# The first feed-forward as seven block products, with the conditioning sums in 512-wide halves

## The chip, the cores and the metric

The kernel runs on one core of a Trainium2 chip. The metric is the device time of one execution in microseconds; single executions are compared by their medians. All numbers below come from one profiled execution of the kernel before, or are stated to come from the timed runs.

## The reference

Two transformer-like blocks work on one sequence of 512 tokens with 1024 features, all in float32. What this case touches is the first block: a conditioning vector `c` is turned into scales, shifts and gates by two layers of weights, and each layer has a feed-forward with 4096 hidden features.

```python
c_act = jax.nn.silu(c)
for i in range(DEPTH):                      # two layers
    mod = c_act @ ada_w[i] + ada_b[i]       # (1024) @ (1024 x 6144)
    sh1, sc1, g1, sh2, sc2, g2 = jnp.split(mod[:, None, :], 6, axis=-1)
    h = rmsnorm(x, norm_g[i, 0]) * (1.0 + sc1) + sh1
    y = mlstm_mixer(h, ...) if i == 0 else sgu_mixer(h, ...)
    x = x + g1 * rmsnorm(y, norm_g[i, 1])
    h = rmsnorm(x, norm_g[i, 2]) * (1.0 + sc2) + sh2
    y = jnp.square(jax.nn.relu(h @ ffn_w1[i])) @ ffn_w2[i]   # 4096 hidden
    x = x + g2 * rmsnorm(y, norm_g[i, 3])
```

Behind it stand a second block (two kinds of attention, a convolutional feed-forward) and a last norm, which the change leaves as they are.

## The kernel before

Float32 products are made from two parts: every operand is split into a high part (`fp32r`) and a rest, and a product of 128x128 by 128x512 takes three matmuls (high x high, high x rest, rest x high). A weight tile of 1 MB lands in `raw`; ScalarE copies it to a high part (`w_both_hi` or `u_both_hi`), VectorE subtracts to get the rest (`..._lo`), and only then TensorE may use it.

The phases stand in a row: `a_in`, the mixer, `a_out`, **ffn0**, `b_in`, `b_out`, **ffn1**, and the second block. There is no scheduler: each engine has its own program written out by hand, in one fixed order, and semaphores tie the programs together. An engine that waits holds back all that stands behind it in its program, DMA issues included.

**ffn0** goes through the 4096 hidden features in four groups of 1024. A group has four weight tiles up (192 matmuls), and four down, in two pairs (`tok_pair`, 192 matmuls). ScalarE squares the rectified hidden block, VectorE makes its rest.

**ffn1** treats its first three groups (`FAST` = 3) another way. The four tiles up are the same (`fast_up`, 192 matmuls, L1264). The product down is cut into 2x2 blocks, and seven block products (`fast_product`, L1282, 168 matmuls) stand for the eight. The operands are sums: T1 = B11+B12 and others of the weights, made by VectorE in the raw tile (`fast_sum`, L2818) and once by an accumulating DMA of GpSimd; S1 to S4 of the hidden blocks, made by VectorE in `s_sum` and `s3_sum` (L2810, L2835, L2844, L2849). Each sum is then split by ScalarE (`fast_a`, L1956; `fast_hi`, L1931) and VectorE (`fast_a_lo`, L2805; `fast_lo`, L2799). The results are added into `Y` by VectorE (`fast_add`, L2829), and the PSUM bank of a product is free only when it has been added. The second product of a group (m = 1) needs both halves of S1, which need the last hidden block of the group. Its order on VectorE is: rest of B11, T1, rest of the first hidden quarter, S3, rest of S3, first half of S1, its rest, rest of T1 (operand 5), T2, second half of S1, its rest. The fourth group of 1024 is done the plain way.

**The conditioning** (`ada`): 48 slices of 256 columns. Slices 20 to 47 (28 slices, in 7 rounds of four) are made during ffn0. ScalarE's program issues a load of 1 MB into the one buffer `ada_raw` (`ada_in`, L1522) when the slice before has been summed; VectorE multiplies and adds eight 128x256 pieces in a row, each waiting for the one before (`ada_sum`, L2210 and L2213). Every four slices TensorE sums over the partitions (`ada_rows4`, L745), ScalarE copies the four rows out (`ada_row_copy`, L1534), TensorE turns them into columns (`ada_turn4`, L752), and VectorE adds the bias (`ada_add4`). The seven rounds stand behind tiles or token blocks of ffn0.

The residual `X` stays in SBUF through both feed-forwards; it goes to memory (`x_dram`) and back once, later, in the second block. SyncE issues all weight loads, and in groups 1 and 2 of ffn0 also 16 writes of 256 KB (`t5_rows`).

## Time and profile before

| | us |
|---|---|
| median of 3 timed runs | 2060.97 |
| lowest and highest of them | 2053.79, 2061.21 |
| the profiled execution | 2058.68 |
| its span in the trace | 2056.9 |
| TensorE busy, share of the span | 2019.9, 98% |
| VectorE, ScalarE busy | 59%, 43% |

The span runs from the first to the last instruction; 1.8 us of the execution lie outside it. "Busy" of TensorE means that some matmul is in flight, so a share of 98% does not say that the matmuls follow each other at their best pace; the distance from start to start says that. The chain that ended last follows the work back from the last instruction, at each step to what released it.

### The profile page before, as it was taken

Reading aid. Unit: us, or ns where it says so; the run is one execution under the profiler, and the core shown is the slowest. Engines: PE = TensorE matmul, PEld = TensorE weight load, DVE = VectorE, ACT = ScalarE, POOL = GpSimd, SP = SyncE. Lnnn points to the kernel's source line nnn. Section 1 sums busy time; section 2 is a strip of 40 time slices with the busy share of each in tenths; the row PEclk is TensorE's granted clock in tenths of the full one; section 3 lists DMA queues with packets and bytes.
Section 4 is the critical chain, followed back from the end, with each engine's and each line's share of the span. In section 5 each row is a group of like instructions: output and inputs, shape, how many; then the busy total and the mean of one; then the engine's idle time right before and its main releaser. Section 6 shows DMA issues by size and latency. Waiting matters only on the chain.

```text
span 2056.9 us, 27536 instructions
## 1 busy us (share of the span) xinstructions
PE 2019.9 (98%) x10822; PEld 1686.5 (82%) x10822; DVE 1223.0 (59%) x1805; ACT 882.6 (43%) x1300; POOL 114.4 (6%) x103
## 2 busy tenths in 40 slices
PE   6999999999999999999999999999999999999998
PEld 4898888888887888988888888876777798888887
DVE  4668857666566345655674735345579736545455
ACT  3333473424247222346454446245455545324233
POOL 0000010000001015100000001000211000000000
PEclk9999999999999999999999999999999999999999
DMA  9562337666553523333434332310132133323321
GB/s 317 164 237 92 116 109 234 196 220 202 184 174 102 164 82 103 96 73 109 161 81 127 123 98 92 121 62 11 57 105 86 42 113 103 103 82 103 103 72 72
DMA packets 225821, 251.52 MB, mean 122 GB/s; under 512 B 11026, under 2 KB 211117, under 8 KB 224805
## 3 DMA queue, kind: packets, MB, share of 16 engines
q1 hardware_dynamic: 181824, 202.45, 31.1%
q10 hardware_dynamic: 42293, 44.27, 6.6%
q0 software_dynamic: 1584, 3.15, 0.9%
q8 instruction: 82, 1.34, 0.3%
q14 instruction: 38, 0.31, 0.0%
HBM read 240.77 MB, written 8.42 MB: 121 GB/s over the span
## 4 chain that ended last, share of the span: by engine, by line
PE 93%; DVE 3%; DMA 1%; ACT 1%; issue 1%; DVEq 1%; SPq 0%; ACTq 0%; POOL 0%; POOLq 0%
PE bank L728 31%; PE bank L800 26%; PE bank L1282 6%; PE bank L1264 5%; PE bank L902 4%; PE bank L1414 4%; PE bank L831 2%; PE bank L972 2%; PE bank L1386 1%; PE bank L1397 1%; PE bank L1116 1%; PE bank L1361 1%; PE bank L1470 1%; PE bank L1455 1%; PE bank L1364 1%; PE bank L1237 1%
## 5 line engine op out<-in xcount | busy, mean ns | idle before, releaser
L728 PE MATMUL bank<-h_hi,w_both_hi 128*128 128x512 f32 x464 | 182.4, 393 | 0.0
L728 PE MATMUL bank<-h_lo,w_both_hi 128*128 128x512 f32 x464 | 181.2, 391 | 0.0
L728 PE MATMUL bank<-h_hi,w_both_lo 128*128 128x512 f32 x464 | 181.1, 390 | 0.0
L2259 DVE TENSOR_TENSOR w_both_lo<-raw,w_both_hi 128x2048 fp32r<-128x2048 f32 x52 | 119.1, 2290 | 68.0 <-ACT w_both_hi L1540 68.0
L2259 DVE TENSOR_TENSOR u_both_lo<-raw,u_both_hi 128x2048 fp32r<-128x2048 f32 x50 | 114.2, 2290 | 76.2 <-ACT u_both_hi L1540 76.2
L1540 ACT ACTIVATE u_both_hi<-raw 128x2048 fp32r<-128x2048 f32 x50 | 94.8, 1907 | 122.4 <-PE bank L800 77.4
L728 PE MATMUL bank<-h_hi,u_both_hi 128*128 128x512 f32 x368 | 143.5, 390 | 0.0
L728 PE MATMUL bank<-h_hi,u_both_lo 128*128 128x512 f32 x368 | 143.2, 389 | 0.0
L728 PE MATMUL bank<-h_lo,u_both_hi 128*128 128x512 f32 x368 | 143.2, 389 | 0.0
L1540 ACT ACTIVATE w_both_hi<-raw 128x2048 fp32r<-128x2048 f32 x50 | 94.8, 1907 | 95.8 <-PE bank L800 44.1
L800 PE MATMUL bank<-u_both_hi,g_hi 128*128 128x512 f32 x312 | 123.5, 396 | 0.0
L800 PE MATMUL bank<-u_both_hi,g_lo 128*128 128x512 f32 x312 | 122.2, 392 | 0.0
L800 PE MATMUL bank<-u_both_lo,g_hi 128*128 128x512 f32 x312 | 122.0, 391 | 0.0
L800 PE MATMUL bank<-w_both_hi,g_hi 128*128 128x512 f32 x280 | 109.4, 391 | 0.0
L800 PE MATMUL bank<-w_both_hi,g_lo 128*128 128x512 f32 x280 | 109.0, 389 | 0.0
L800 PE MATMUL bank<-w_both_lo,g_hi 128*128 128x512 f32 x280 | 108.9, 389 | 0.0
L728 PEld LDWEIGHTS bank<-h_hi,w_both_hi 128*128 128x128 f32 x464 | 87.4, 188 | 19.3 <-issue 1.5
L728 PEld LDWEIGHTS bank<-h_hi,w_both_lo 128*128 128x128 f32 x464 | 87.5, 189 | 18.4
L728 PEld LDWEIGHTS bank<-h_lo,w_both_hi 128*128 128x128 f32 x464 | 87.5, 189 | 18.3 <-issue 0.2
L2213 DVE SCALAR_TENSOR_TENSOR ada_acc<-ada_raw,c_act,ada_acc 128x256 f32<-128x256 f32 x182 | 88.3, 485 | 14.2 <-issue 0.6
L2202 DVE TENSOR_TENSOR w_both_lo<-raw,w_both_hi 128x2048 fp32r<-128x2048 f32 x29 | 67.3, 2321 | 39.9 <-ACT w_both_hi L1514 39.5
L728 PEld LDWEIGHTS bank<-h_hi,u_both_lo 128*128 128x128 f32 x368 | 69.1, 188 | 14.5
(504 smaller groups left out, 5089.8 us busy)
## 6 DMA issues: line engine op xcount, KB each, us to landing
raw<-in_ffn_w SPq DMA_DIRECT2D x64, 1024.0 KB, 5.3
ada_raw<-in_ada_w ACTq DMA_DIRECT2D x40, 1024.0 KB, 5.2
raw<-in_w_up SPq DMA_DIRECT2D x22, 1024.0 KB, 5.1
raw<-in_b_w_in SPq DMA_DIRECT2D x16, 1024.0 KB, 5.4
raw<-in_w_in SPq DMA_DIRECT2D x15, 1024.0 KB, 5.5
raw<-in_a_w_in SPq DMA_DIRECT2D x12, 1024.0 KB, 6.2
ada_head<-in_ada_w SPq DMA_DIRECT2D x8, 1024.0 KB, 12.2
raw<-in_b_w_out SPq DMA_DIRECT2D x8, 1024.0 KB, 7.2
```

The source lines that it names most:

```text
L728: mm = pe.matmul(o, x, y, start=(k == 0 and j == 0), stop=(k == kc - 1 and j == 2))
L800: mm = pe.matmul(bank[c][:].rearrange("p (s n) -> p s n", s=2), x, y, start=(k == 0 and j == 0), stop=(k == kc - 1 and j == 2))
L831: mm = pe.matmul(bank[c][:, s * 256:s * 256 + 256], x, y[:, k], start=(k == 0 and j == 0), stop=(k == KB - 1 and j == 2))
L902: mm = pe.matmul(bank[2 * s + b][:, hs], x, y, start=(k == 0 and j == 0), stop=(k == KB - 1 and j == 2))
L972: mm = pe.matmul(bank[6][:], x, y, start=(k == 0 and j == 0), stop=(k == KB - 1 and j == 2))
L1264: mm = pe.matmul(bank[m][:], x[:, k, bs], y[:, k], start=(k == i == 0), stop=(k == KB - 1 and i == 2))
L1282: mm = pe.matmul(o[:], x[:, k, cs], y[:, k], start=(k == i == 0 and begins), stop=(k == 3 and i == 2), skip_group_check=True)
L1414: mm = pe.matmul(bank[7][:], x, y, start=(k == 0 and j == 0), stop=(k == KB - 1 and j == 2))
L1540: act.activation(slot(where, s)[0], raw[s][:], ACT.Copy).then_inc(sem("hi_done"), 1)
L2202: dve.tensor_tensor(w_lo[s][:], raw[s][:], f32(w_hi[s][:]), ALU.subtract).then_inc(sem("split_done"), 1)
L2213: i = dve.scalar_tensor_tensor(o, src[:, k], c_act[:, k:k + 1], o, ALU.mult, ALU.add)
L2259: dve.tensor_tensor(lo, raw[s][:], f32(hi), ALU.subtract).then_inc(sem("split_done"), 1)
```

## The change

Both feed-forwards now run through one function `ffn(st, name, came_from)` on each engine, with three groups of seven products and a plain fourth group. All semaphore counts get a term for the stage `st`. In detail:

- The fast scheme is in ffn0. The sixth product uses PSUM banks 6 and 7 (before, in ffn1: 4 and 5), since 4 and 5 serve the conditioning.
- `X` is written to `x_dram` at the start of each feed-forward and read back behind the last block product, in front of the boundary that adds to it; `s_sum`, `s3_sum` and one slot of split operands lie in its place.
- The conditioning slices 20 to 47 become 14 units of 512 columns, each in two halves of four 128x512 pieces: 28 halves of 1 MB in one buffer `ada_half` (where `ada_raw` was). ScalarE issues the load of half n (`ada_load(n)`) when half n-1 has been summed (`ada_half_sum`), each at a fixed place among its activations. Halves 0 to 23 are placed in ffn0 (5, 6 and 6 in the three fast groups, 7 in the last one), 24 to 27 in groups 1 and 2 of ffn1. The sums rotate over three accumulators.
- Of the seven rounds of row sums, five stand in ffn0, one in `b_in`, one in ffn1.
- SyncE's load of `ws_raw` waits for the sixth round; TensorE waits for its bias before it turns `ws_raw`.

```diff
-PHASES = [("a_in", 12, 2), ("a_out", 4, 2), ("ffn0", 32, 2), ("b_in", 16, 2), ("b_out", 8, 2), ("ffn1", 10, 2),
+PHASES = [("a_in", 12, 2), ("a_out", 4, 2), ("ffn0", 10, 2), ("b_in", 16, 2), ("b_out", 8, 2), ("ffn1", 10, 2),
...
+                        sp.wait_ge(sem("xs_ready"), NC * (BOUNDS[came_from] + 1))
+                        sp.dma_start(x_dram, X[:].rearrange("p c d -> p (c d)")).then_inc(sem("x_out"), 16)
...
+                        sp.wait_ge(sem("f_product"), fast_made(st, FAST - 1, 6, 1))
+                        sp.dma_start(X[:].rearrange("p c d -> p (c d)"), x_dram).then_inc(sem("x_in"), 16)
...
+                for j in range(4):
+                    tile(t0 + 2 + j, j % 2, q0 + 1 + j // 2, h_hi, h_lo, parts=slot("WU"[j // 2], j % 2),
+                         added=fast_added(st, FAST - 1, 6, 0) if j == 0 else None)
+                    if st == 0 and j == 0:
+                        ada_rows4(3)
+                    if st == 0 and j == 1:
+                        ada_turn4(3)
+                    if st == 0 and j == 3:
+                        ada_rows4(4)
+
+                def turned(c):
+                    if st == 0 and c == 1:
+                        ada_turn4(4)
...
+                if i == 0:
+                    ada_rows4(5)
+                if i == 1:
+                    ada_turn4(5)
...
+            def ada_load(n):
+
+                col0, layer = (n // 2 * 512 + 5120, 0) if n < 4 else (n // 2 * 512 - 1024, 1)
+                act.wait_ge(sem("ada_summed"), 20 + n)
+                act.dma_start(ada_half[:], cols(A["ada_w"][layer], col0, 512)[:, n % 2 * 4:n % 2 * 4 + 4, :])\
+                    .then_inc(sem("ada_late"), 16)
...
+                    fast_s(st, g, 1)
+                    fast_a(st, g, 4, s3_sum)
+                    if st == 0:
+                        ada_load(6 * g + 2)
+                    fast_hidden(st, q0, g, 4)
+                    fast_hidden(st, q0, g, 5)
...
+            def ada_half_sum(n):
+
+                unit, half = n // 2, n % 2
+                o = acc_ring[unit % 3]
+                if half == 0 and unit >= 3:
+                    dve.wait_ge(sem("ada_rows_mm"), 5 + (unit - 3) // 2)
+                dve.wait_ge(sem("ada_late"), 16 * (n + 1))
+                for k in range(4):
+                    which = c_act[:, 4 * half + k:4 * half + k + 1]
+                    if half == k == 0:
+                        i = dve.tensor_scalar(o, ada_half[:, k], which, None, ALU.mult)
+                    else:
+                        dve.drain()
+                        i = dve.scalar_tensor_tensor(o, ada_half[:, k], which, o, ALU.mult, ALU.add)
+                i.then_inc(sem("ada_summed"), 1)
...
+                    if st == 0:
+                        ada_half_sum([16, 17, 19, 20, 22, 23][j])
...
+                    if st == 0 and j in (1, 3):
+                        ada_half_sum(18 if j == 1 else 21)
```

**VectorE, one plain group up.** Before, in ffn0, a weight rest, then a conditioning sum, then the rests of two hidden blocks (`g_lo`), and again:

```order
L2259 TENSOR_TENSOR w_both_lo<-raw_56,w_both_hi 128x2048 [waits hi_done]
L2210 TENSOR_SCALAR ada_acc_c<-ada_raw,c_act 128x256 [waits ada_in]
L2213 SCALAR_TENSOR_TENSOR ada_acc_c<-ada_raw,c_act,ada_acc_c 128x256 x7
L2669 TENSOR_TENSOR g_lo<-tmp_80,g_hi 128x512 [waits ffn_ghi]
L2669 TENSOR_TENSOR g_lo<-tmp_81,g_hi 128x512 [waits ffn_ghi]
L2259 TENSOR_TENSOR w_both_lo<-raw_57,w_both_hi 128x2048 [waits hi_done]
```

Now, in group 1 of ffn0: half 5, a weight rest, halves 6 and 7 with the bias of round 0 between them, then the rest of B11 (`w_both_lo`), T1 (`raw_56<-raw_56,raw_57`), and S3 (`s_sum<-g_full`):

```order
L2241 SCALAR_TENSOR_TENSOR ada_acc<-ada_half,c_act,ada_acc 128x512 [waits ada_late]
L2241 SCALAR_TENSOR_TENSOR ada_acc<-ada_half,c_act,ada_acc 128x512 x3
L2692 TENSOR_TENSOR u_both_lo<-raw_64,u_both_hi 128x2048 [waits f_hi]
L2238 TENSOR_SCALAR ada_acc_s<-ada_half,c_act 128x512 [waits ada_late,ada_rows_mm]
L2241 SCALAR_TENSOR_TENSOR ada_acc_s<-ada_half,c_act,ada_acc_s 128x512 x3
L2248 TENSOR_TENSOR mods<-bank,vcols 128x8 [waits ada_mm]
L2408 TENSOR_TENSOR ycol<-mods,vcols 128x8
L2241 SCALAR_TENSOR_TENSOR ada_acc_s<-ada_half,c_act,ada_acc_s 128x512 [waits ada_late]
L2241 SCALAR_TENSOR_TENSOR ada_acc_s<-ada_half,c_act,ada_acc_s 128x512 x3
L2692 TENSOR_TENSOR w_both_lo<-raw_56,w_both_hi 128x2048 [waits f_hi]
L2711 TENSOR_TENSOR raw_56<-raw_56,raw_57 128x2048 [waits part_in1]
L2698 TENSOR_TENSOR a_lo_67<-g_full,a_hi_66 128x1024 [waits f_a_hi]
```

The sums now stand in front of the operands of the block products.

**ScalarE, last group of ffn0.** Before, in the first group, a load stands behind the four hidden blocks and again behind the next two:

```order
L1522 DMA ada_raw<-in_ada_w 128x8x256 [waits ada_summed]
L1540 ACTIVATE w_both_hi<-raw_56 128x2048 [waits block_done,tile_in0]
L1811 ACTIVATE tmp_80<-bank 128x512 [waits block_done,ffn_g]
L1813 ACTIVATE tmp_80<-tmp_80 128x512
L1815 ACTIVATE g_hi<-tmp_80 128x512
```

Now, from the end of the first plain tile (half 17) over halves 18 and 19 to the copy of the row sums of round 3 (`ada_row`):

```order
L1870 DMA ada_half<-in_ada_w 128x4x512 [waits ada_summed]
L1548 ACTIVATE u_both_hi<-raw_57 128x2048 [waits block_done,tile_in1]
L1870 DMA ada_half<-in_ada_w 128x4x512 [waits ada_summed]
L1958 ACTIVATE tmp_82<-bank 128x512 [waits block_done,ffn_g]
L1960 ACTIVATE tmp_82<-tmp_82 128x512
L1962 ACTIVATE g_hi<-tmp_82 128x512
L1958 ACTIVATE tmp_83<-bank 128x512 [waits block_done,ffn_g]
L1960 ACTIVATE tmp_83<-tmp_83 128x512
L1962 ACTIVATE g_hi<-tmp_83 128x512
L1870 DMA ada_half<-in_ada_w 128x4x512 [waits ada_summed]
L1548 ACTIVATE w_both_hi<-raw_56 128x2048 [waits block_done,tile_in0]
L1542 ACTIVATE ada_row_118<-bank 128x256 [waits ada_mm,ada_rows_mm]
```

The copy of round 3 stands behind two loads that each wait for the sum of the half before.

## Rows read from the trace of the kernel before

**Rows 1.** The page: busy time of the engines; TensorE clock granted, in 40 slices.
```profile
PE 2019.9 (98%) x10822; PEld 1686.5 (82%) x10822; DVE 1223.0 (59%) x1805; ACT 882.6 (43%) x1300; POOL 114.4 (6%) x103
...
PEclk9999999999999999999999999999999999999999
```

**Rows 2.** Chain that ended last, in ffn0: start us, us, what, matmuls.
```profile
300.64 21.79 PE bank L728 x96
...
338.74 0.57 PE bank L745 x8
...
344.99 0.34 PE bank L752 x4
```

**Rows 3.** The same chain in ffn1: one group of seven products.
```profile
1008.14 43.52 PE bank L1264 x192
1051.66 38.08 PE bank L1282 x168
```

**Rows 4.** Busy us (instructions) in ffn0, ffn1 and one group; clock, DMA share.
```profile
300.60:628.70 328.10, 328.10 (x1494) 267.72 (x1493) 216.21 (x343) 121.66 (x145) 2.40 (x3) 1.00 0.63 199
948.30:1250.90 302.60, 302.60 (x1337) 250.49 (x1337) 185.76 (x156) 141.59 (x148) 6.38 (x6) 1.00 0.38 113
1008.10:1089.70 81.60, 81.60 (x362) 67.57 (x361) 52.17 (x40) 37.33 (x35) 1.29 (x1) 1.00 0.39 116
```

**Rows 5.** VectorE in order of time, ffn0: start us, us, what [idle before].
```profile
301.79 0.35 DVE L2210 TENSOR_SCALAR ada_acc_c<-ada_raw,c_act 128x256 f32<-128x256 f32 x1
302.22 3.84 DVE L2213 SCALAR_TENSOR_TENSOR ada_acc_c<-ada_raw,c_act,ada_acc_c 128x256 f32<-128x256 f32 x7
...
311.16 0.35 DVE L2210 TENSOR_SCALAR ada_acc_c<-ada_raw,c_act 128x256 f32<-128x256 f32 x1 [0.34 <-DMA ada_raw<-in_ada_w]
```

**Rows 6.** ScalarE in order of time, ffn0, same columns.
```profile
306.09 0.37 ACTq L1522 DMA_DIRECT2D ada_raw<-in_ada_w  x1
...
339.38 0.38 ACT L1534 ACTIVATE ada_row<-bank 128x256 f32<-128x256 f32 x1 [2.83 <-PE bank L745]
```

**Rows 7.** The tile ada_raw from 300 to 652 us, 27 loads.
```profile
DMA to landing us min/median/max: 5.0/5.1/7.1
```

**Rows 8.** VectorE groups by line: busy us, mean ns of one.
```profile
L2324 DVE SCALAR_TENSOR_TENSOR x_res<-y_acc,r,x_res 128x512 f32<-128x512 f32 x32 | 22.6, 749 | 5.7 <-POOL r L3138 5.3
...
L2979 DVE TENSOR_SCALAR tmp<-tmp,soft 128x512 f32<-128x512 f32 x32 | 15.6, 487 | 2.8 <-issue 0.4
```

**Rows 9.** VectorE in order of time, ffn1, second group.
```profile
1033.07 2.29 DVE L2799 TENSOR_TENSOR w_both_lo<-raw,w_both_hi 128x2048 fp32r<-128x2048 f32 x1 [8.59 <-ACT w_both_hi L1931]
...
1038.80 1.22 DVE L2835 TENSOR_TENSOR s_sum<-g_full 128x1024 f32<-128x1024 f32 x1
...
1049.09 2.29 DVE L2818 TENSOR_TENSOR raw<-raw,raw 128x2048 f32<-128x2048 f32 x1
...
1054.42 0.69 DVE L2805 TENSOR_TENSOR a_lo<-s_sum,a_hi 128x512 fp32r<-128x512 f32 x1 [0.70 <-ACT a_hi L1956]
```

**Rows 10.** ScalarE in order of time, the same stretch.
```profile
1040.05 1.06 ACT L1956 ACTIVATE a_hi<-s_sum 128x1024 fp32r<-128x1024 f32 x1 [5.87 <-DVE s_sum L2835]
...
1052.36 0.63 ACT L1945 ACTIVATE g_full<-tmp 128x512 f32<-128x512 f32 x1
```

**Rows 11.** Windows of a_out, columns as in rows 4.
```profile
251.00:253.00 2.00, 2.00 (x6) 1.58 (x5) 1.90 (x5) 2.00 (x3) 0.00 (x0) 0.52 0.00 0
```

**Rows 12.** Chain that ended last, in a_out.
```profile
247.91 0.96 PE bank L1167 x2
248.87 16.14 PE bank L800 x63
```

**Rows 13.** DMA issues: count, KB each, median us to landing.
```profile
raw<-in_ffn_w POOLq DMA_DIRECT2D x3, 1024.0 KB, 8.6
...
x_rows<-x_res SPq DMA_DIRECT2D x1, 2048.0 KB, 7.7
```

**Rows 14.** ScalarE in order of time, b_in.
```profile
685.83 0.63 ACT L1859 ACTIVATE v_all<-tmp 128x512 f32<-128x512 f32 x1 [4.81 <-DVE tmp L2725]
```

## What is expected of the change

> **What bounds the kernel now.** I read the page first: TensorE is busy 98% of the span at full clock [rows 1]. Then the chain of waits, for the pace. In ffn1 a group is 192 matmuls up in 43.52 us and 168 down in 38.08 [rows 3], both 0.2267 us from start to start, with no gap: there the matmuls alone set the time, and the seven products hide all that VectorE and ScalarE do for them. In ffn0 the same pace is broken only by the small matmuls of the conditioning, 0.57 and 0.34 us [rows 2]. The windows give ffn0 328.1 us and ffn1 302.6 for the same piece of work [rows 4]: the 25.5 between them are the 72 matmuls that ffn1 saves (16.3) and 9.2 for seven conditioning rounds (1.3 each). So what must be asked is whether TensorE still finds its operands ready in ffn0 when the conditioning stands among them.
>
> **What is saved.** 3 x (192 - 168) = 72 matmuls at 0.2267 us: -16.3 us. All on the path. Of the seven rounds of small matmuls two only change their phase: 0.
>
> **The price of a half.** It has 128x512 pieces, which the trace has not in this operation. Nearest rows: the 512-wide multiply-add takes 749 ns, the 512-wide multiply 487 ns [rows 8]; between dependent pieces 0.06 us pass (seven of 0.485 us in 3.84) [rows 5]. A first half is 0.49 + 3 x 0.75 + 0.2 = 2.9 us, a second one 4 x 0.75 + 0.2 = 3.2, so 3.1 on the average. A load of 1 MB lands 5.1 us after its issue, 5.0 to 7.1 [rows 7]. With one buffer the load waits for the sum and the sum for the load: 5.1 + 3.1 + 0.1 = 8.3 us per half at best. (The same loop takes 9.4 us before, from 301.79 to 311.16 [rows 5], with sums of 4.2.) VectorE is busy 52.2 of 81.6 us in a group [rows 4]; six halves add 18.6. By the average there is room. But both engines take their programs in order, and the loop of 8.3 us stands in front of what the block products need.
>
> **The second product of each group.** Group 1, counted from its first matmul up. The load of half 4 goes out at about -0.5, behind the sum of half 3. It is summed by 7.5; half 5 by 15.9; half 6 by 24.0. The load of half 7 stands on ScalarE behind the hidden blocks of the second tile, which is done at 21.8 plus 1.3 of small matmuls plus 1.2 for the two activations: 24.3; summed at 32.7. Only then come the rest of B11, T1, the rest of the first hidden quarter and S3 (2.2, 2.4, 1.1 and 1.2 us by [rows 9]): S3 at 39.6, where ffn1 has it at 31.9 (1038.80 + 1.22 against 1008.14) [rows 3, 9]. ScalarE splits it (1.06 [rows 10]) and issues half 8 at 40.6. VectorE has half 8 in front of operand 5: landed 45.7, summed 48.6, then the rest 50.8, T2 53.2, and second half of S1, its split and its rest (0.7 each) 55.3. TensorE wants it at 43.5 + 1.3 + 5.4 = 50.3. It waits 5.0 us. In ffn1 the last rest ends at 1055.1 and is wanted at 1051.66 + 5.44 = 1057.1 [rows 3, 9]: 2.0 us of slack, so nothing of this wait is covered. Group 0 has two halves in front of S3 and the third before operand 5: half 0 summed 13.7 us after its start, half 1 at 22.1, S3 29.0, half 2 landed 35.3, S1 complete 44.9 against 39.5: 5.3. Group 2 is like group 1 with other small matmuls: 4.5. Together **14.8**. Bounds: with landings of 5.0 it is about 14; with 7.1 in every load of the loop it passes 30; in the other direction, if the halves took no longer than before's free gaps allow, 0.
>
> **The ends of the groups.** Half 3, 9 and 15 stand in front of the last sum-out, on which the next tile waits. By the durations of [rows 9] for the rests and 0.6 us per sum-out, VectorE reaches them only some 3 us before the deadline; a half of 3.2 and the sum-out overshoot by 0.7, 0.7 and, with the bias of round 2, 2.4: **3.8** us (bounds 1 and 6).
>
> **The turn of round 3.** TensorE turns it behind the second plain tile; the row copy stands on ScalarE behind the loads of halves 18 and 19. From the end of the first plain tile: activations 1.9, landing 5.1, half 17 3.2, landing 5.1, half 18 2.9, issue 0.5, a split 1.9, the copy 0.4 [rows 6], 0.3 of hand-overs: 21.3. TensorE has meanwhile 10.9 + 0.8 = 11.7 us of work. It waits **9.6** (9.2 at the fastest landings, 13.6 at the slowest).
>
> **The turn of round 4.** It stands behind the second token block down; the copy stands behind the load of half 23, so behind the sum of half 22. From the end of the third plain tile: 2.0, three landings 15.3, halves 20 to 22 9.1, 1.0 for issue and copy: 27.4; TensorE has 10.9 + 0.8 + 10.9 = 22.6: **4.8** (4.5 to 10.8).
>
> **The turn of round 5, in b_in.** TensorE turns right behind a pair of token blocks; the copy stands behind the gelu of the last block. Sum-out 0.7, gelu 0.63 [rows 14], copy 0.38 [rows 6]: **1.7**.
>
> **The clock.** Behind 1 us and more of small matmuls in a_out the granted clock was 0.52, between its two levels, 1.2 and 2.4 GHz, and 63 matmuls took 16.14 us in place of 14.3 [rows 11, 12]: 1.9 lost. Five waits of 4 to 10 us could each cost that, 9.5; but a slow product lets VectorE catch up, so part comes back from the ends of groups, and shorter waits may pass. I take **5** (0 to 9.5). The Trainium skill (TensorE: Matmul & The Clock Gate, section on why this matters for kernels) names idle gaps between bursts of matmuls as what sends the clock back; by it all five would count, and the sum would be 4 us higher.
>
> **At no cost.** Parking X: 2 MB out took 7.7 us to land [rows 13]; S3 of group 0, the first to write there, comes 28 us into the group, while X is written from about its start, and the way back starts with 87 us of matmuls ahead. The accumulating DMA (8.6 us [rows 13]) starts at T1, some 7 us later than in ffn1, and its operand is the fifth product's: wanted 28 us later. ffn1 gets two halves in each of two groups, done before S3: 0. Some loads queue behind SyncE's: **+2** (0 to 8).
>
> **The sum.** 2058.7 (the profiled execution) - 16.3 + 14.8 + 3.8 + 9.6 + 4.8 + 1.7 + 5 + 2 = 2084.1. The median of the runs lies 2.3 above that execution, inside their spread of 7.4, so I leave it at **2084**.
>
> **Rivals.** (1) All waits vanish in the slack that the averages show, and the 72 matmuls are gained: 2058.7 - 16.3 = 2042 (faster). For it: 29 us of idle VectorE per group [rows 4]. Against: a loop of 8.3 us per half is latency, not busy time, and sits before operands with 2.0 us of slack. (2) The group waits are hidden after all, because halves run much ahead of what I count, and only the fixed turns stay: 2058.7 - 16.3 + 9.6 + 4.8 + 1.7 + 3.8 = 2062 (no change). It decides at whether half 7 is summed before 25 us of its group. (3) Loads collide: the halves share the DMA engines with weight tiles, writes of 256 KB and the parked X; at landings of 6 us on the average the three group waits become 8 each and the turns 13 and 8, with the whole of the clock 2100. The DMA share of 0.63 in ffn0 [rows 4] speaks for some of it, the median of 5.1 under that same load against. The Trainium skill (Trainium Kernel Development and Optimization, Key Constraints) says that DMAs of all queues run on the same 16 engines and that another issuing engine saves issue time alone; by it ScalarE's issuing gives no relief. (4) The scheme not doing what it says: the order shows 168 matmuls per group as in ffn1; I give it nothing.
>
> **How the numbers follow.** Forecast 2084 (2072 to 2095): 0.68. Rival 3: 0.15. Rival 2: 0.10. Rival 1: 0.07. The range 2068 to 2100 leaves out rival 1, most of rival 2 and the end of rival 3. Faster by over 0.5%, about what a measurement can tell: 0.07; within 0.5%: 0.10; slower: 0.83.
>
> **What would show it.** TensorE waiting on `a_lo` or `f_a_lo` before the second product of each group, 4 to 6 us; on `ada_row` twice in the plain group, about 10 and 5 us; ffn0 some 20 us longer where the matmuls fell by 72; ffn1 unchanged but for 1.3. Wrong: a half-sum well under 3 us, a half landing in under 4, or group 1 without a wait.

## The result, and the profile after

| | before | after |
|---|---|---|
| median of the runs, us | 2059.4 | 2107.7 |
| lowest and highest | 2053.8, 2061.2 | 2104.5, 2110.9 |
| the profiled execution | 2058.68 | 2104.52 |
| its span | 2056.9 | 2102.7 |

The ratio is 1.0239, with a 95% interval of 1.0213 to 1.0266. The forecast was 2084 (2068 to 2100): slower, as it came, but by half of what was measured.

Three windows of each kernel split the program at the same places: from the second half of ffn0's first pair of tiles to the next phase, then to the same place in ffn1, then to the end of that. Columns as in [rows 4]. First before, then after:

```profile
288.36:652.08 363.72, 362.95 (x1700) 297.70 (x1701) 236.27 (x371) 149.76 (x196) 5.91 (x8) 1.00 0.60 189
652.08:935.99 283.91, 283.27 (x1473) 242.99 (x1473) 144.44 (x165) 102.72 (x133) 50.34 (x32) 1.00 0.37 110
935.99:1274.37 338.38, 337.68 (x1593) 283.30 (x1593) 204.83 (x183) 168.31 (x199) 9.88 (x11) 1.00 0.36 107
```

```profile
284.98:695.80 410.82, 357.76 (x1605) 291.62 (x1605) 272.82 (x287) 171.14 (x203) 9.87 (x11) 0.93 0.56 172
695.80:983.96 288.16, 285.19 (x1485) 243.63 (x1485) 144.67 (x166) 103.07 (x134) 50.38 (x32) 1.00 0.35 110
983.96:1323.38 339.42, 338.99 (x1605) 283.82 (x1605) 216.51 (x201) 168.84 (x200) 9.73 (x11) 1.00 0.44 130
```

ffn0 became 47.1 us longer, b_in and b_out 4.3, ffn1 1.0 (its round of small matmuls). The stretches outside are 6.6 us shorter (3.4 ahead, 3.2 behind). The change touches nothing there: with the same program ahead of it, ffn0's window begins anywhere from 284.7 to 288.9 us in the profiles of this case, so that is the difference of two executions. In ffn0 TensorE is idle for 53 us where it was idle for 0.8, and the granted clock of the stretch is 0.93. What it waited for from 280 to 740 us, which takes in ffn0 and the start of b_in (total us, times, longest):

```profile
PE bank L1208 <- issue: 27.5, 3, 9.4
PE bank L758 <- ACT ada_row L1542: 26.3, 3, 18.6
...
PE bank L733 <- DVE y_acc L2722: 0.2, 1, 0.2
```

and the same waits one by one, in order of time, with the idle time before each in brackets:

```profile
333.59 0.77 PE L1208 MATMUL bank<-u_both_hi,a_hi 128*128 128x512 f32 x1 [9.10 <-issue]
...
428.78 0.77 PE L1208 MATMUL bank<-w_both_hi,a_hi 128*128 128x512 f32 x1 [9.07 <-issue]
...
524.41 0.77 PE L1208 MATMUL bank<-w_both_hi,a_hi 128*128 128x512 f32 x1 [9.36 <-issue]
...
601.25 1.02 PE L758 MATMUL bank<-cst_sb,ada_row 128*128 128x4 f32 x4 [18.59 <-ACT ada_row L1542]
...
644.54 1.02 PE L758 MATMUL bank<-cst_sb,ada_row 128*128 128x4 f32 x4 [5.99 <-ACT ada_row L1542]
...
731.24 0.61 PE L758 MATMUL bank<-cst_sb,ada_row 128*128 128x4 f32 x4 [1.72 <-ACT ada_row L1542]
```

They are the waits of the prediction, at its places: before the second block product of each group, at the turns of rounds 3 and 4, and in b_in at that of round 5. Two sizes differ. The chain that ended last shows why, for group 1 (start us, us, what):

```profile
407.73 1.15 DVE s_sum L2749
...
408.90 9.77 DMA ada_half<-in_ada_w
...
421.35 0.75 DVE ada_acc_c L2241
...
427.98 0.69 DVE a_lo L2698
```

and for the plain group:

```profile
572.48 14.60 DMA ada_half<-in_ada_w
...
600.83 0.38 ACT ada_row L1542
```

TensorE's first matmul of group 1 stands here:

```profile
368.48 0.39 PE L1190 MATMUL bank<-h_hi,u_both_hi 128*128 128x512 f32 x1
```

So S3 was ready 40.4 us into the group (408.88), where the prediction had 39.6, and the load of half 8 went out at that moment, where the prediction had 40.6. TensorE wanted the second product at 51.2 (428.78 less the wait of 9.07), where the prediction had 50.3. Up to that point the working holds to within 1 us. Then the load took 9.77 us and not 5.1. The other transfers of the stretch say what was in flight (count, KB, median us to landing):

```profile
ada_half<-in_ada_w ACTq DMA_DIRECT2D x24, 1024.0 KB, 5.2
...
raw<-in_ffn_w POOLq DMA_DIRECT2D x3, 1024.0 KB, 10.0
...
x_res<-x_rows SPq DMA_DIRECT2D x1, 2048.0 KB, 17.2
...
gy_rows<-ycol SPq DMA_DIRECT2D x1, 4.0 KB, 19.7
```

The median of the 24 loads is 5.2, beside 5.1 in [rows 7]. But halves 2, 8 and 14 start 1.8 to 2.0 us behind GpSimd's accumulating DMA (T1 ends at 406.6 in group 1). Half 17, issued at 572.5, stands beside X coming back and the write of `gy_rows`, both issued at 560, and beside two weight tiles issued at 562 and 565, which took 20.1 and 22.0 us. That gives the theories:

- **A**, collisions: the sum of the prediction is right but for the landings of these four loads.
- **F**, order: the copies of the row sums wait on ScalarE behind loads that they don't need.
- **H**, place: the latencies of the halves can all stand where nothing waits for them, and then the seven products pay.
- Rivals: **D**, the busy time of VectorE's sums is what costs; **G**, 24 halves at 8.3 us leave no place in 340 us without a wait.

### The profile page after: what moved, and what is told of

It reads as the page before. It is cut to its first block, busy times and chain, and to the rows that moved or that the text cites. A ratio compares the mean times of both kernels' runs of the same rounds, so it can differ in the third digit from the quotient of the medians.

```text
span 2102.7 us, 27080 instructions
## 1 busy us (share of the span) xinstructions
PE 2014.5 (96%) x10750; PEld 1679.7 (80%) x10750; DVE 1271.5 (60%) x1740; ACT 905.3 (43%) x1309; POOL 118.2 (6%) x106
## 4 chain that ended last, share of the span: by engine, by line
PE 77%; DVE 9%; DMA 7%; ACT 3%; DVEq 1%; issue 1%; ACTq 1%; SPq 0%; POOL 0%; POOLq 0%
PE bank L733 25%; PE bank L806 18%; PE bank L1208 5%; DMA ada_half<-in_ada_w 5%; PE bank L1190 5%; PE bank L1422 4%; PE bank L908 3%; PE bank L978 2%; PE bank L1394 1%; PE bank L1405 1%; PE bank L1122 1%; PE bank L837 1%; DVE ada_acc_c L2241 1%; PE bank L1369 1%; DVE raw L2711 1%
## 5 line engine op out<-in xcount | busy, mean ns | idle before, releaser
L2283 DVE TENSOR_TENSOR w_both_lo<-raw,w_both_hi 128x2048 fp32r<-128x2048 f32 x42 | 96.2, 2290 | 50.6 <-ACT w_both_hi L1548 50.5
L1208 PE MATMUL bank<-w_both_hi,a_hi 128*128 128x512 f32 x224 | 89.6, 400 | 18.4 <-issue 18.4
L733 PE MATMUL bank<-h_lo,u_both_hi 128*128 128x512 f32 x272 | 106.8, 393 | 0.0
L733 PE MATMUL bank<-h_hi,u_both_lo 128*128 128x512 f32 x272 | 106.8, 393 | 0.0
L2692 DVE TENSOR_TENSOR w_both_lo<-raw,w_both_hi 128x2048 fp32r<-128x2048 f32 x40 | 91.5, 2288 | 21.6 <-ACT w_both_hi L1836 21.5
L1836 ACT ACTIVATE w_both_hi<-raw 128x2048 fp32r<-128x2048 f32 x40 | 76.4, 1910 | 56.5 <-PE bank L1208 22.8
L2208 DVE TENSOR_TENSOR w_both_lo<-raw,w_both_hi 128x2048 fp32r<-128x2048 f32 x29 | 67.3, 2321 | 39.1 <-ACT w_both_hi L1522 38.6
L1548 ACT ACTIVATE w_both_hi<-raw 128x2048 fp32r<-128x2048 f32 x38 | 71.7, 1905 | 44.6 <-PE bank L806 27.5
L1208 PE MATMUL bank<-w_both_lo,a_hi 128*128 128x512 f32 x224 | 89.1, 398 | 0.0
L1208 PE MATMUL bank<-w_both_hi,a_lo 128*128 128x512 f32 x224 | 88.8, 396 | 0.0
L806 PE MATMUL bank<-u_both_hi,g_hi 128*128 128x512 f32 x216 | 84.9, 393 | 0.0
L806 PE MATMUL bank<-u_both_hi,g_lo 128*128 128x512 f32 x216 | 84.2, 390 | 0.0
L806 PE MATMUL bank<-u_both_lo,g_hi 128*128 128x512 f32 x216 | 84.0, 389 | 0.0
```

The source lines that it names most:

```text
L733: mm = pe.matmul(o, x, y, start=(k == 0 and j == 0), stop=(k == kc - 1 and j == 2))
L806: mm = pe.matmul(bank[c][:].rearrange("p (s n) -> p s n", s=2), x, y, start=(k == 0 and j == 0), stop=(k == kc - 1 and j == 2))
L1208: mm = pe.matmul(o[:], x[:, k, cs], y[:, k], start=(k == i == 0 and begins), stop=(k == 3 and i == 2), skip_group_check=True)
L1548: act.activation(slot(where, s)[0], raw[s][:], ACT.Copy).then_inc(sem("hi_done"), 1)
L1836: act.activation(fast_slot(11 * g + i)[0], f_raw[fast_raw(g, name)][:], ACT.Copy).then_inc(sem("f_hi"), 1)
L2208: dve.tensor_tensor(w_lo[s][:], raw[s][:], f32(w_hi[s][:]), ALU.subtract).then_inc(sem("split_done"), 1)
```

## The experiments

Each changed ffn0 alone; placed3 and those built on it also move one copy in b_in. "Wait" is idle time of TensorE. The kernel before had a median of 2056.7 to 2057.8 beside them.

### The collisions one by one

**acc_late.** GpSimd starts the accumulating DMA when the load beside it has landed.

```diff
                 pool.wait_ge(sem("f_sum"), fast_summed(st, g, "T1"))
+                if st == 0:
+                    pool.wait_ge(sem("ada_late"), 16 * (6 * g + 3))
```

> The changed kernel with one more wait: in the first feed-forward GpSimd starts its accumulating DMA only when the load of half 2, 8 or 14 has landed (both started within a microsecond of each other before). Theory A (collision: each of these loads lands after 9.5 to 9.8 us only because it shares the way with the accumulating DMA): these three land in 5.1 to 5.7 us, TensorE's waits before the second product of each group fall from 9.1, 9.1 and 9.4 us to 4.5 to 5.3 each, -12 to -14 us in all: 2094 to 2096 us. The operand of the accumulating DMA is wanted more than 20 us later, so its delay costs nothing. Rival B (the three loads are slow for another reason, the weight tiles of SyncE or the queue of ScalarE): landings stay at 9.5 us, the time stays at 2107, or rises where the later accumulation is missed.

Measured: 2092.5 us, ratio 1.0172 (1.0150 to 1.0194): 15 us less, somewhat more than the 12 to 14 of A. In its profile, which is of the slowest of its executions (2098.4), the waits before the second products fell less than A has it (the lines of L1208; the 11.9 are 6.8 and 5.1):

```profile
PE bank L1208 <- issue: 11.9, 2, 6.8
PE bank L1208 <- DVE a_lo L2698: 7.4, 1, 7.4
...
raw<-in_ffn_w POOLq DMA_DIRECT2D x3, 1024.0 KB, 8.5
```

In both_apart below they were 6.9, 5.6 and 5.1. That is more than 5.3, since some halves ahead of them now landed in 6.8 to 8.0 us. The accumulating DMA itself went from 10.0 to 8.5 us. B falls. The wait at the turn of round 3 stayed (19.8 us): there half 16 was issued together with the write of `gy_rows` and took 17.3 us.

**x_back_late.** X is read back behind the landing of half 23 (`sp.wait_ge(sem("ada_late"), 16 * 24)` ahead of the same DMA).

> The changed kernel with the read-back of the 2 MB of X in the first feed-forward moved behind the landing of half 23 (some 70 us later, 30 us before X is wanted). Theory A (collision with the read-back made the load of half 17 take 14.6 us): that load lands in 5.1 to 6 us, TensorE's wait for the copy of round 3 falls from 18.6 us to 9 to 10, the wait of round 4 stays at 5 to 6: -9 us, 2098 to 2099 us. Rival B (the load is slow because of weight tiles or the write of gy_rows beside it): landing and wait stay, 2107. Rival C (the read-back comes too late at its new place): the first addition to X waits for it in the boundary, and the 9 us are lost there.

Measured: 2104.1 us, 1.0233 (1.0211 to 1.0255). X landed in 7.9 us, nothing waited for it, but half 17 still took 9.3 us and the wait was 13.5, not 9 to 10. So the larger transfer was only about half of the cause.

```profile
573.59 9.29 DMA ada_half<-in_ada_w
```

**both_apart.** Both edits.

> Both edits together: accumulating DMA behind the load of halves 2, 8, 14, and X read back behind half 23. Theory A (my sum of the prediction was right but for the landings of these four loads): waits 4.5 to 5.3 three times, 9 to 10 and 5 to 6 in the plain group, 2084 to 2087 us. Rival (the loop of loads and sums is longer by more than these collisions, or the collisions move on to other loads): over 2092.

Measured: 2091.6 us, 1.0170 (1.0146 to 1.0195), 4.6 above the range of A and under that of its rival. Half 17 took 8.9 us, the turn waited 13.0.

**gy_late.** The write of `gy_rows` goes behind half 23 as well.

> The kernel both_apart with one more move: the write of gy_rows (4 KB in 1024 pieces of 4 bytes, 13 to 20 us) also goes behind the landing of half 23, with X. In x_back_late and both_apart the load of half 17 still took 9.3 and 8.9 us with X out of the way. Theory A2 (the small pieces of gy_rows hold back the load of half 17): it lands in 5.1 to 5.7 us, TensorE's wait for the copy of round 3 falls from 13.0 to 9.2 to 9.8 us, 2087 to 2089 us against 2091.6 of both_apart. Rival E (the load is slow beside the weight tile of SyncE, or needs 9 us there anyway): 8.9 us and 13.0 us stay, 2091 to 2092.

Measured: half 17 landed after 5.24 us and the wait was 9.28, where the prediction had 9.6. But the time was 2098.7 us, 1.0200 (1.0183 to 1.0217), since a new wait came in the last pair of token blocks:

```profile
563.24 5.24 DMA ada_half<-in_ada_w
...
582.70 1.01 PE L763 MATMUL bank<-cst_sb,ada_row 128*128 128x4 f32 x4 [9.28 <-ACT ada_row L1547]
...
625.79 1.02 PE L763 MATMUL bank<-cst_sb,ada_row 128*128 128x4 f32 x4 [5.87 <-ACT ada_row L1547]
...
664.58 1.94 PE L878 MATMUL bank<-cst_sb,y_acc 128*128 128x128 f32 x8 [10.84 <-ACT y_acc L1587]
```

SyncE waits for the write before it reads the row back, and stood there for 11 us; its next weight tile then took 10.8 us beside X, and ScalarE, in order, waited for that tile. The theory held and the edit cost more than it gave.

**no_collisions.** The accumulating DMA behind the load, X in four pieces behind the weight tiles down, and `gy_rows` in eight DMAs of 128 pieces of 4 bytes:

```diff
+                    if st == 0 and g == 2:
...
+                        sp.dma_start(gy_dram[1].rearrange("(k p) -> p k", p=P)[:, j:j + 1], ycol[:, 1, j:j + 1],
...
+                    if st == 0:
+                        sp.dma_start(X[:, j], x_dram[:, j * D:j * D + D]).then_inc(sem("x_in"), 16)
```

> The changed kernel with its order of the halves, copies and turns untouched and the three collisions taken away: the accumulating DMA behind the load of halves 2, 8 and 14; X read back in four pieces of 512 KB behind the weight tiles down; gy_rows written in eight pieces of 128 x 4 bytes, one behind each write of 256 KB in the third group. Theory A (the sum of the prediction was right in its waits but for the landings that these collisions made): waits of 5 to 7 us three times before the second products, 9.2 to 10 and 5.7 us in the plain group, 0 in the last pair: 2084 to 2089 us. Rival (the pieces now slow other loads by as much): 2092 and over.

Measured: 2115.5 us, 1.0281 (1.0267 to 1.0295), the slowest of all. The last pair had no wait any more, so the pieces of X are good; but each small DMA took about as long as the whole write had (11.1 to 17.2 us), and beside them three halves took 10.7 to 15.0 and weight tiles up to 22.1 us. The DMA issues of ffn0, and one of the halves in the chain:

```profile
gy_rows<-ycol SPq DMA_DIRECT2D x8, 0.5 KB, 14.6
```

```profile
455.42 15.04 DMA ada_half<-in_ada_w
```

The turn of round 2 waited 19.5 us. So the harm does not shrink with the bytes that one DMA moves: 512 bytes in 4-byte pieces did as much as 4 KB.

**no_collisions2.** The row is turned first: TensorE transposes the 128x8 columns (`pe.transpose(bank[5][0:KB, 128:256], ycol[:, 1], ident)`), VectorE copies the 8 rows, SyncE writes them in one DMA of 8 pieces of 512 bytes in the third group, among the weight tiles that the small DMAs had stood beside. The rest is as in no_collisions.

> The changed kernel with its order of halves, copies and turns untouched; the accumulating DMA behind the load of halves 2, 8 and 14; X read back in four pieces of 512 KB; and gy_rows no longer written in pieces of 4 bytes: TensorE turns the 128x8 columns into 8 rows of 128 (one small matmul, 0.1 us), VectorE copies them, SyncE writes 8 pieces of 512 bytes in the third group. In no_collisions the eight DMAs of 128 x 4 bytes took 14.6 us each, and the loads beside them 10.7 to 15.0 us. Theory K (a DMA of 4-byte pieces holds back all loads beside it by some 10 us whatever its bytes; in rows of 512 bytes it doesn't): no half takes over 8 us, TensorE waits 5 to 7 us three times, 9.2 to 10 and 5.6 us, as my sum had it: 2084 to 2089 us. Rival L (the place in the third group is what hurts, whatever the form): a half of 10 us and more there, over 2095.

Measured: 2083.6 us (2082.0 to 2089.8), 1.0136 (1.0116 to 1.0156). No half took over 7.04 us.

```profile
328.94 0.77 PE L1218 MATMUL bank<-u_both_hi,a_hi 128*128 128x512 f32 x1 [4.71 <-issue]
...
420.49 0.77 PE L1218 MATMUL bank<-w_both_hi,a_hi 128*128 128x512 f32 x1 [4.96 <-issue]
...
512.66 0.76 PE L1218 MATMUL bank<-w_both_hi,a_hi 128*128 128x512 f32 x1 [5.17 <-issue]
...
582.20 1.02 PE L768 MATMUL bank<-cst_sb,ada_row 128*128 128x4 f32 x4 [11.14 <-ACT ada_row L1552]
...
624.17 1.02 PE L768 MATMUL bank<-cst_sb,ada_row 128*128 128x4 f32 x4 [5.52 <-ACT ada_row L1552]
```

The first three add up to 14.8, the number of the prediction. That the sum fits to the tenth is partly luck: half 7 took 6.5 us here. Half 18 took 7.04, 1.9 more than in the working, and the turn of round 3 waited 11.1. This is the change as the prediction had it before its eyes, with its order untouched: theory A stands, L and the rival of no_collisions fall.

### Latency or work

**no_loads.** Halves 1 to 23 aren't loaded; all sums work on the data of half 0.

```diff
+                if 0 < n < 24:
+                    return
                 act.wait_ge(sem("ada_summed"), 20 + n)
...
-                dve.wait_ge(sem("ada_late"), 16 * (n + 1))
+                dve.wait_ge(sem("ada_late"), 16 * (n - 22) if n >= 24 else 16)
```

> The changed kernel in which the loads of halves 1 to 23 are left out; the 24 sums, row sums, copies and turns of the first feed-forward stay and all work on the data of half 0. Theory A (what costs is the latency of a chain load, sum, load, sum): with landings of 0 the waits before the second products vanish, the copy of round 3 comes some 4 us late at most: 2058.7 - 16.3 + 0 to 5 = 2042 to 2048 us. Rival D (the busy time of the 512-wide sums on VectorE in front of the operands is what costs): waits of 4 us and more before the second products stay, and the time is over 2065.

Measured: 2055.2 us, 0.9989 (0.9979 to 1.0000). The three waits before the second products fell to 1.4 us and twice to under 0.3 with every sum in its place, so D falls:

```profile
PE bank L758 <- ACT ada_row L1542: 7.0, 2, 5.3
PE bank L1208 <- issue: 1.4, 1, 1.4
...
532.68 18.15 DMA raw<-in_ffn_w
```

It was 7 to 13 us above what A expected. 5.3 of that is the turn of round 3, which waited with no half in flight, with some 3 us of slow clock behind it: the last row shows a weight tile of SyncE beside X and `gy_rows`, the same collision on another victim. The turn of round 5 in b_in, which A's range had left out, made 1.7 and some 1.5 of slow clock.

### Order and place

**turns_early** is gy_late with the copy of round 3 ahead of the load of half 17, and halves 20 to 23 behind the fourth hidden pair.

```diff
-                        ada_load([17, 19, 20, 22][j])
+                    if st == 0 and j == 0:
+                        ada_row_copy(3)
+                    if st == 0 and j in (0, 1, 3):
+                        ada_load({0: 17, 1: 19, 3: 20}[j])
```

> The kernel gy_late with another order in the plain group alone: ScalarE copies the row sums of round 3 in front of the load of half 17 (they are ready by then), and the loads and sums of halves 20 to 23 stand behind the fourth hidden pair. Theory F (the waits of rounds 3 and 4 are made by the order of ScalarE's program, which puts the copies behind loads that wait for other halves): both waits go, 9.5 and 5.7 us, with some 2 us each of slow clock behind them; the waits before the second products stay at 5 to 7 us: 2069 to 2074 us. Rival G (seven halves in the plain group take 8.3 us each whatever the order, so the waits come back before the token blocks, on the weight rests or on the hidden blocks): over 2080.

Measured: 2101.3 us, 1.0208 (1.0191 to 1.0225). Both waits at the turns were gone; in the last pair there was one of 30.1 us. That is in G's range. But part of it was SyncE, as in gy_late; the next kernel puts that part right.

**turns_early2**, with X in four pieces and `gy_rows` in one write in the third group:

> The kernel turns_early with SyncE's part put right: there and in gy_late the write of gy_rows came so late that SyncE, waiting for it, issued the first weight tiles of the next phase late, and TensorE waited 10.8 and 30.1 us in the last pair of token blocks. Now gy_rows is written in the third group, when half 10 has landed, and X is read back in four pieces of 512 KB, one behind each weight tile down of the plain group. Theory F (the two turns in the plain group waited because of ScalarE's order alone): no wait over 2 us from the end of the third group to the next phase, the waits before the second products stay (5.5 to 7 us each): 2066 to 2071 us. Rival G (the seven halves of 8.3 us each and the pieces of X collide, and waits of 5 us and more come back before the token blocks): over 2075.

Measured: 2096.1 us, 1.0187 (1.0170 to 1.0204): F is right about the two waits and wrong about the gain, G has most of it. The last pair still waited 14.1 us, behind the loads of halves 22 and 23, which ScalarE now reached at its end; and the write of `gy_rows` at its new place made one half take 19.4 us and the turn of round 2 wait 12.5. A wait taken from one spot of a chain of loads and sums came up at the chain's end.

**placed** is gy_late with all 24 halves, their loads, the row sums, copies and turns at new places. These were worked out by following all four engines' programs in order with the durations of the rows, until hardly a wait was left. In group 1, for instance, VectorE has halves 5 and 6 among the weight rests, 7 behind S3, 8 behind the second half of S1 and 9 behind the rest of operand 8; and the turn of round 3 comes half a tile later. The count of halves in ffn0 is the same.

> The kernel gy_late with the 24 halves, their loads, the row sums, copies and turns of the first feed-forward at other places: a half stands in each group where VectorE would wait for a weight tile, for instance half 2 behind the first sum-out of the second product and not in front of operand 5, and each row copy behind activations that have nothing to wait for; the number of halves in the first feed-forward is the same. Theory H (all of the loss is the place of the latencies, none of it the work): waits of at most 1 to 2 us each remain, 5 to 10 in all with 0 to 4 of slow clock: 2045 to 2056 us, not slower than the kernel before. Rival G (24 halves of 8.3 us in 340 us leave no place without a wait): waits over 20 us in all, over 2065.

Measured: 2073.0 us, 1.0078 (1.0061 to 1.0095). The waits in the groups were 0.4 to 0.8 us, 2.3 in all; but SyncE's late write, inherited from gy_late, made 17.5 us in the last pair, and the first token block waited 3.5. By time and by the sum of its waits this is in G's range; the next kernel takes SyncE's part out.

**placed2** (the same with X in pieces and `gy_rows` in one early write of 4-byte pieces):

> The kernel placed with the same two moves of SyncE (gy_rows in the third group, X in four pieces behind the weight tiles down). In placed TensorE waited 17.5 us in the last pair of token blocks and 3.5 us before the first; all other waits in the first feed-forward were under 1 us. Theory H: the 17.5 us and 1.5 to 2 us of slow clock behind them go: 2073 - 19 = 2052 to 2056 us. Rival I (the pieces of X now collide with halves 19 to 23, and their time comes back before the token blocks): the 3.5 us there grow to 8 and more, 2060 and over.

Measured: 2057.5 us, 1.0006 (0.9995 to 1.0018): 15.5 us gained where 17 to 21 were expected, and I falls, since the wait before the first token block was 2.1. In its profile, of an execution of 2063.4 us, half 11 took 16.7 us beside the write, with a wait of 3.5 us in the third group. **placed3** moves some halves on, and the copy of round 5:

> As placed2, with the halves and rounds at slightly other places (the loads at the end of the third group and in the plain group leave more room before the first token block) and, in the next phase, the copy of round 5 moved from behind the last gelu of its step to behind the second. Theory H: no wait before the first token block (3.5 us in placed with 1.7 us of slow clock), none before the turn of round 5 (1.7 us, and 1.6 of slow clock behind it): 2045 to 2050 us, faster than the kernel before by 0.3 to 0.6%. Rival: the small waits stay in other places, 2052 to 2056, no different from before.

Measured: 2056.3 us, 0.9993 (0.9984 to 1.0003), the rival. Two waits of 2.5 and 2.6 us in the third group stood behind a weight tile of 15.3 us, in flight when the write of `gy_rows` was issued at 444.8, and a half of 11.0, issued 11.9 us behind it. The trace has no landing for that write.

```profile
441.40 15.25 DMA raw<-in_ffn_w
...
456.68 11.01 DMA ada_half<-in_ada_w
```

**placed4** writes it in eight small DMAs, as no_collisions did:

> The kernel placed3 with gy_rows written in eight pieces as in no_collisions. In placed3 the one write of 1024 pieces of 4 bytes stood beside a weight tile that took 15.3 us and a half that took 11.0 us, and TensorE waited 2.5 and 2.6 us behind them, with 2.4 to 3 us of slow clock. Theory J (a write of 4-byte pieces holds back every load beside it; in eight parts it holds back each by 1 to 2 us, which the slack takes): both waits and their clock go, 2048 to 2051 us, ratio 0.995 to 0.997 to the kernel before. Rival (no gain from the pieces): 2056.

Measured: 2069.8 us, 1.0057 (1.0043 to 1.0071): J falls, a half took 22.3 us and a wait of 13.3 us came at the start of the third group. **placed5** writes rows of 512 bytes, two weight tiles further on than placed3, where placed4's small DMAs stood too:

> placed3 with gy_rows written as 8 rows of 512 bytes in the third group. Theory K: the two waits of 2.5 us in the third group and the slow clock behind them go: 2048 to 2051 us, ratio 0.995 to 0.997. Rival L: no difference from placed3, 2056.

Measured: 2047.6 us (2046.8 to 2049.2), 0.9957 (0.9944 to 0.9971), **faster than both kernels**, and 8.6 us under placed3: K stands, L falls. Its waits in ffn0:

```profile
PE bank L1233 <- DVE y_acc L2755: 2.3, 3, 0.9
PE bank L887 <- ACT y_acc L1586: 2.2, 1, 2.2
PE bank L1233 <- DVE y_acc L2753: 1.0, 1, 1.0
```

and the stretches that stood above at 410.8 and 288.2:

```profile
286.80:640.86 354.06, 347.41 (x1606) 283.83 (x1606) 271.80 (x288) 170.49 (x203) 9.87 (x11) 1.00 0.63 200
640.86:926.00 285.14, 284.51 (x1485) 243.63 (x1485) 144.64 (x166) 103.01 (x134) 50.36 (x32) 1.00 0.35 110
```

VectorE and ScalarE are as busy there as in the changed kernel (271.8 and 272.8, 170.5 and 171.1 us): the same work in ffn0, 56.8 us shorter. H stands, G falls. The part of placement alone is 36.0 us: that lies between no_collisions2 (2083.6) and placed5, which treat the accumulating DMA, X and `gy_rows` alike. ffn0 is 9.7 us shorter than before, of the 16.3 that the 72 matmuls are worth.

**placed6** moves some halves once more:

> placed5 with other places for some halves (the last loads a little earlier, to free ScalarE before the last pair of token blocks, where TensorE waited 2.1 us in placed3). If that wait goes and none comes: 2046 to 2050 us, a ratio of 0.994 to 0.997. If the small waits only move: as placed5.

Measured: 2050.7 us, 0.9970 (0.9958 to 0.9982), just outside what was expected and not apart from placed5 in its interval. The 2.2 us in the last pair were gone, and 4.1 stood before a product of the third group. Small waits only moved.

## Why the prediction was right in its direction and wrong in its size

| term | forecast | measured in ffn0 or b_in | difference |
|---|---|---|---|
| 72 matmuls less | -16.3 | the same count | 0 |
| second products | 14.8 | 9.1 + 9.1 + 9.4 = 27.5 | +12.7 |
| ends of groups | 3.8 | 0.2 | -3.6 |
| turn of round 3 | 9.6 | 18.6 | +9.0 |
| turn of round 4 | 4.8 | 6.0 | +1.2 |
| turn of round 5 | 1.7 | 1.7 | 0 |
| clock | 5 | 13.7 | +8.7 |
| loads queueing | 2 | part of the above | -2 |
| rest of b_in, b_out and ffn1 | 0 | 1.0 | +1.0 |
| outside the change | 0 | -6.6 | -6.6 |

The differences make 20.4: 2084.1 + 20.4 = 2104.5, the profiled execution. The 1.0 holds a wait of 0.6 us in b_out behind a weight tile that landed in 9.5 us.

**The steps that failed.** Two landings, both put at what a load takes in [rows 7]. One is "landed 45.7", the 5.1 us of halves 2, 8 and 14; they took 9.5 to 9.8. The other is "At no cost": "Parking X", with the write of `gy_rows` beside it; half 17 took 14.6. The term that should have held them, "some loads queue behind SyncE's", was +2. The clock, at 5, was the third term too small, at 13.7.

**The price of a half.** Right. The pieces take 0.75 us, 0.83 from start to start (420.52 to 421.35), and from the load of half 5 to that of half 6 it was 8.5 us (376.82 to 385.34) where the prediction had 8.3.

**The second products.** The mechanism and the place were right, and in group 1 all times up to the load's issue held to within 1 us; the term that failed is "landed 45.7", the landing of 5.1 us for halves 2, 8 and 14. The bounds of 5.0 to 7.1 came from [rows 7], where no load stood beside an accumulating DMA. The prediction placed that DMA in time ("starts at T1") and asked only whether its own operand comes in time, not whose load starts beside it. Rival 3 had the right kind of cause but spread it: 6 us on the average, where the median stayed at 5.2 and four loads of 24 took 9.5 to 14.6. (Its own 13 us for the turn of round 3 is also too much: two landings at 0.9 more each make 9.6 into 11.4.) Groups 0, 1 and 2 were forecast at 5.3, 5.0 and 4.5; without the collision they are 4.7, 5.0 and 5.2.

**The ends of groups.** Too much by 3.6. It is likely that a TensorE that has stood for 5 to 9 us lets VectorE catch up, so that the term before pays for this one; in no_collisions2, with waits of 5 us, it was 0, and in no_loads, with hardly a wait before it, there were 0.7 and 0.4. No run tests it by itself.

**Rounds 3 and 4.** The order argument was right: 9.3 and 5.9 in gy_late, 11.1 and 5.5 in no_collisions2. The failing step stands under "At no cost": "Parking X". The prediction asked whether X is back in time and not what 2 MB coming back do to the load beside them; and it did not list SyncE's write of `gy_rows`, which the change moved into the plain group. Each was about half of the cause: without X half 17 took 9.3 us in place of 14.6, without both 5.2; no run moves the write alone. The kernel before had a hint of it. There the write was issued at 594.2 us, 1.4 us behind the load of the last slice, and that load took 7.07 us: it is the 7.1 of [rows 7], against a median of 5.1.

**The clock.** Forecast 5; 13.7 is what is left in ffn0: 47.1 + 16.3 + 2.6 (two rounds of 1.3 went to later phases) - 52.3 of waits. Counted by the slow matmuls behind the five waits it is some 13. All five waits cost, as the Trainium skill's section named in the prediction has it (TensorE: Matmul & The Clock Gate, why this matters for kernels), and the trace agrees in kind; the price in [rows 12], 1.9 us, was too small. Behind the wait of 9.36:

```profile
524.41 0.77 PE L1208 MATMUL bank<-w_both_hi,a_hi 128*128 128x512 f32 x1 [9.36 <-issue]
...
525.40 0.63 PE L1208 MATMUL bank<-w_both_hi,a_lo 128*128 128x512 f32 x1
525.82 0.63 PE L1208 MATMUL bank<-w_both_hi,a_hi 128*128 128x512 f32 x1
...
529.54 0.40 PE L1208 MATMUL bank<-w_both_hi,a_hi 128*128 128x512 f32 x1
529.77 0.40 PE L1208 MATMUL bank<-w_both_lo,a_hi 128*128 128x512 f32 x1
```

The matmuls start 0.43 us apart in place of 0.227, at a granted clock of 0.50 from 525 to 529 us, the level of 1.2 GHz: 12 of them take 5.1 us and not 2.7, 2.4 lost. Behind the turn of round 3 it was 3.3, behind that of round 4 2.3. The prediction took 4.5 off for "a slow product lets VectorE catch up"; if that came back, it did so in the 3.6 us of the ends of groups and not here.

**A forecast met by offsets.** no_collisions2 came to 2083.6 beside a forecast of 2084, but not term by term: its waits are 33.2 us beside 34.7, its clock costs some 14 us beside 5 (the remainder, as above), and the stretch ahead of ffn0 was 3.6 us shorter than in the profile of before. The waits are what it confirms.

## What to carry to other kernels

Before a load is put beside other transfers, list everything that any queue starts within some 10 us of it, the 4 KB ones too, and take the landing from a row with the same company. When an order of work waits on latencies, moving one wait only passes it on; what helped was to place the whole chain of loads and sums so that each sum stands where its engine is free and each hand-over has nothing unneeded ahead of it. And a wait of TensorE can cost more than its length: the five waits of 6 us and more in the changed kernel's ffn0 cost 2.3 to 3.3 us more each, while behind those of 1 us and less in placed5 no matmul ran slow.

## What the runs showed of the hardware

- A DMA to memory in pieces of 4 bytes slowed the loads issued beside it. 4 KB in 1024 such pieces took 10.7 to 19.7 us; issued together with it or behind it while it was in flight, halves took 8.9 to 19.4 us in place of 5.2, and weight tiles up to 21.0 (turns_early2), or 22.3 where X came back as well (acc_late). A load already in flight was slowed less: half 16 took 5.1, 6.6 and 8.4 us where it was issued 1.0, 0.4 and 0.8 us ahead of the write (changed kernel, x_back_late, both_apart). Eight DMAs of 512 bytes in 4-byte pieces took 14.6 us each (median) and slowed five loads of the chain to 10.7 to 15.0. With the same 4 KB in 8 pieces of 512 bytes no half took over 7.04 us (no_collisions2); how long that write itself took the trace doesn't have. The Trainium skill (DMA: Bandwidth & Descriptors, issuing engines are not separate DMA queues) says that DMAs of all engines run on the same 16 DMA engines; the trace agrees, since slowed loads were ScalarE's and the write was SyncE's.
- An accumulating DMA and a plain load of 1 MB each, started together: 10.0 and 9.5 to 9.8 us, where they take 8.5 and 5.2 apart.
- A wait of 1.7 us can be enough for the clock to fall, and need not be. Twelve kernels have the same wait of 1.72 us at the turn of round 5, at the same place of the same program. In six profiles the matmuls ran slow behind it, with some 1.5 us lost (x_back_late, both_apart, gy_late, no_loads, turns_early2, placed); in the other six, the changed kernel's among them, they did not. Windows of placed, where the turn ended at 697.8, and one of the changed kernel, where it ended at 731.9 (last three columns: granted clock, DMA share, GB/s):

```profile
696.00:700.00 4.00, 2.82 (x12) 2.41 (x13) 1.23 (x2) 2.70 (x3) 0.00 (x0) 0.86 1.03 426
700.00:704.00 4.00, 4.00 (x14) 3.10 (x14) 1.25 (x1) 0.00 (x0) 0.00 (x0) 0.71 0.86 263
...
732.00:736.00 4.00, 4.00 (x19) 3.27 (x18) 2.29 (x1) 0.99 (x1) 0.00 (x0) 1.00 0.93 338
```

With that copy moved (placed5) the stretch of b_in and b_out lost 3.0 us against the changed kernel: 1.7 of this wait, 0.6 of the one in b_out, and 0.7 for which no cause is shown.
